# First tiles of the output projection and of the merge computed inside the cores, scores and squares in other gaps, an eviction's place, and norms' halves added on GpSimd

## What is computed

```
hn = rms_norm(h, ln_mix[0]);  h += gdn_mixer(hn)            # gated delta rule, 8 heads
h += swiglu(rms_norm(h));     h += ple gate                 # PLE = p @ w * sigmoid(rms_norm(h) @ w)
k, v = shared_kv(h);          h += sb_mixer(rms_norm(h))    # stick-breaking attention, 8 heads
h += swiglu(rms_norm(h));     h += ple gate
x = h;  x += 0.5 * swiglu(rms_norm(x))
y_hy = hyena_branch(...)      # filters from a small MLP, divided by their norm, DFT as matmuls
y_rw = rwkv7_branch(...)      # token shift, recurrence per head in both directions, group norm, gate
x += (sigmoid(g_hy) * y_hy @ hy_out + sigmoid(g_rw) * y_rw @ rw_out) @ w_out
x += 0.5 * swiglu(rms_norm(x));  out = rms_norm(x)
```

## Time and profile before

| what | value |
|---|---|
| time, median of 3 runs | 3155.7 us (3154.51 to 3155.88) |
| profiled execution, its own time | 3157.63 us |
| its span, first to last instruction | 3155.8 us |
| PE busy | 2996.7 us, 95% of the span |
| DVE, ACT, POOL busy | 48%, 34%, 7% |
| chain that ended last, by engine | PE 81%, DVE 5%, ACT 4%, issue 2% |
| mean granted TensorE clock | 0.98 |

### The profile page before, as it was taken

The page is one execution under the profiler, slowest core; times in us unless marked ns, Lnnn a source line. Parts: engine busy times, 40 slices in busy tenths (PEclk is TensorE's granted clock), DMA queues, the critical chain, the costliest instruction groups (busy, mean ns, idle before and its releaser), DMA issues.

```text
span 3155.8 us, 46998 instructions
## 1 busy us (share of the span) xinstructions
PE 2996.7 (95%) x21374; PEld 2461.1 (78%) x21374; DVE 1502.1 (48%) x1435; ACT 1058.5 (34%) x1115; POOL 215.8 (7%) x125
## 2 busy tenths in 40 slices
PE   8988889999999889999999999989998998999998
PEld 6767768888788778888878888768877887788886
DVE  6654534443354444443354434445567664544432
ACT  4453333222344333222342222432244332232221
POOL 1002100000000000000010000320002211000000
PEclk9999989999999999999999999989999999999999
DMA  3210012223222102222322223312230002122222
GB/s 137 80 57 2 2 54 94 93 94 114 98 92 84 51 15 93 102 99 100 107 88 99 94 95 117 104 44 90 77 126 4 3 5 111 67 94 102 99 94 80
DMA packets 44758, 249.29 MB, mean 79 GB/s; under 512 B 8428, under 2 KB 12268, under 8 KB 16913
## 3 DMA queue, kind: packets, MB, share of 16 engines
q1 hardware_dynamic: 43408, 242.11, 21.8%
q10 hardware_dynamic: 1152, 4.19, 0.3%
HBM read 237.90 MB, written 8.39 MB: 78 GB/s over the span
## 4 chain that ended last, share of the span: by engine, by line
PE 81%; DVE 5%; ACT 4%; issue 2%; POOL 0%; DVEq 0%; ACTq 0%
PE ps L560 65%; PE ps L2613 7%; PE ps L1319 2%; PE ps L1947 1%; PE ps L2223 1%; PE ps L2207 1%; ACT whi L265 1%; DVE wlo L271 1%; DVE gdn_XX L1661 0%; PE ps L3396 0%; PE ps L2799 0%; PE ps L1379 0%; DVE sb_sp L3496 0%; ACT sb_la L3470 0%; PE ps L1470 0%
## 5 line engine op out<-in xcount | busy, mean ns | idle before, releaser
L271 DVE TENSOR_TENSOR wlo<-wraw,whi 128x2048 fp32r<-128x2048 f32 x210 | 487.0, 2320 | 1000.3 <-ACT whi L265 1000.1
L265 ACT ACTIVATE whi<-wraw 128x2048 fp32r<-128x2048 f32 x210 | 402.1, 1915 | 1006.1 <-PE ps L560 1006.1
L560 PE MATMUL ps<-ffn_xh,whi 128*128 128x512 f32 x1408 | 550.4, 391 | 2.2 <-DVE ffn_xl L380 2.1
L560 PE MATMUL ps<-ffn_xh,wlo 128*128 128x512 f32 x1408 | 552.2, 392 | 0.0
L560 PE MATMUL ps<-ffn_xl,whi 128*128 128x512 f32 x1408 | 549.5, 390 | 0.0
L560 PEld LDWEIGHTS ps<-ffn_xh,whi 128*128 128x128 f32 x1408 | 264.4, 188 | 60.3 <-DVE ffn_xl L380 2.5
L560 PEld LDWEIGHTS ps<-ffn_xl,whi 128*128 128x128 f32 x1408 | 264.3, 188 | 60.0 <-issue 0.7
L560 PEld LDWEIGHTS ps<-ffn_xh,wlo 128*128 128x128 f32 x1408 | 264.5, 188 | 55.7
L560 PE MATMUL ps<-ffn_uh,wlo 128*128 128x512 f32 x704 | 275.9, 392 | 0.0
L560 PE MATMUL ps<-ffn_uh,whi 128*128 128x512 f32 x704 | 275.5, 391 | 0.0
L560 PE MATMUL ps<-ffn_ul,whi 128*128 128x512 f32 x704 | 274.2, 389 | 0.0
(11 more groups left out here) (494 smaller groups left out, 4747.9 us busy)
## 6 DMA issues: line engine op xcount, KB each, us to landing
wraw<-in_weights SPq DMA_DIRECT2D x212, 1024.0 KB, 4.8
gates_kept<-gates_tmp ACTq DMA_DIRECT2D x8, 512.0 KB, 4.1
mix_gate<-gates_kept SPq DMA_DIRECT2D x8, 512.0 KB, 11.2
h<-in_x SPq DMA_DIRECT2D x4, 512.0 KB, 7.9
mix_y<-hz_kept SPq DMA_DIRECT2D x2, 1024.0 KB, 5.9
out<-out SPq DMA_DIRECT2D x4, 512.0 KB, 2.7
ple_raw<-in_p SPq DMA_DIRECT2D x4, 256.0 KB, 5.1
hy_decay<-in_hy_decay SPq DMA_DIRECT2D x4, 256.0 KB
```

The source lines that it names most:

```text
L265: c.nc.scalar.activation(c.whi[:, j % 2, :], c.wraw[:, j % 2, :], ACT.Copy).then_inc(c.hi_ready, 1)
L271: c.nc.vector.tensor_tensor(c.wlo[:, j % 2, :], c.wraw[:, j % 2, :], c.whi[:, j % 2, :].bitcast(F32), ALU.subtract).then_inc(c.lo_ready, 1)
L560: last = nc.tensor.matmul(pair[:, m, :], a, b, start=opens and n == 0 and wa + xa == 0, stop=closes and n == len(ks) - 1 and wa == 1)
```

## The change

Seven parts.

1. **Norms.** After the last accumulation POOL adds the two halves of `norm_acc` (a new 128x512 addition, `one`), in all ten norms. `pe_sum` waits for it and multiplies one half instead of two; in `kv_n` four sums per token instead of eight.
2. **Units.** `Dense.tensor` is cut into units (three matmuls of one 128-wide block of one k), which `tensor_ahead` can issue from another part. `skip_group` twice keeps the parity of the PSUM pairs for `gdn_out`.
3. **Gated delta rule.** In stage GP slots 8 to 19 issue one unit each of tile 0 of `gdn_out` (heads 0 to 5), stage GP+1 slots 1 to 4 three units each of tile 1: 24 units. The casts of the two held tiles move from slots 6 and 12 of stage GP to slots 1 and 3.
4. **Hyena filter.** The squares of the second filter on ACT move from after the last tile of `project` to beside tile 4 and early in tile 5; PE sums them after tile 0 of `gates` instead of halfway through it.
5. **Recurrence.** The last slots of DVE's preparation of pair 0 (19 and on) move from tile 6 to tile 7 of `shift`, behind the last eviction.
6. **Merge.** In the last stage of `Recurrence` 14 of the 16 units of the merge's tile 0 are issued, 6 at slot 0, 3 at 17, 3 at 19, 2 at 21.
7. **Attention.** Scores and softplus of heads 0 and 1 stand beside tiles 2 and 3 of `v_part`; the core's loop starts at head 0. `o` and `w` get other places in SBUF.

```diff
+def skip_group(c):
+    c.freed[c.groups] = c.freed[c.groups - 2]
+    c.groups += 1
...
+            if q == (2 if self.direct else 3):
+                pool.wait_ge(*self.Q.at(f"{name}.acc{q}"))
+                nc.gpsimd.tensor_tensor(b.acc[:, 0, :], b.acc[:, 0, :], b.acc[:, 1, :], ALU.add)\
+                    .then_inc(*self.Q.done(f"{name}.one"))
...
-        pe.wait_ge(*self.Q.at(f"{name}.acc{2 if self.direct else 3}"))
+        pe.wait_ge(*self.Q.at(f"{name}.one"))
...
-        for m in range(2):
-            last = nc.tensor.matmul(c.ps[:, 4, :], c.ones[:, :], b.acc[:, m, :], start=m == 0,
-                                    stop=m == 1 and not self.direct)
+        last = nc.tensor.matmul(c.ps[:, 4, :], c.ones[:, :], b.acc[:, 0, :], start=True, stop=not self.direct)
...
+    def tensor_ahead(self, pe, r, end):
+        for unit in self.units(r)[self.begun.get(r, 0):end]:
+            self.pe_unit(pe, r, *unit)
+        self.begun[r] = end
...
# DeltaCore.tensor, .scalar, .vector
+                if stage == GP and 8 <= s < 20:
+                    self.out.tensor_ahead(pe, 0, s - 7)
+                elif stage == GP + 1 and 1 <= s < 5:
+                    self.out.tensor_ahead(pe, 1, (3, 6, 9, 12)[s - 1])
...
-                if stage == GP and s in (6, 12):
-                    ring_lo(c, dve, self.j_held - 2 + s // 12)
+                if stage == GP and s in (1, 3):
+                    ring_lo(c, dve, self.j_held - 2 + s // 3)
...
# HyenaFilters
+            self.act_square(act, 1, 0)
+            self.act_square(act, 1, 1)
         elif r == 5:
-            for q in range(NH):
-                self.act_square(act, 1, q)
+            self.act_square(act, 1, 3)
             self.act_norm(act, 1)
...
     def tensor_halfway(self, pe, r):
-        if r == 0:
-            f.pe_squares(pe, 1)
...
# Recurrence
+                if k == HP + 1 and s in (0, 17, 19, 21):
+                    self.merge.tensor_ahead(pe, 0, {0: 6, 17: 9, 19: 12, 21: 14}[s])
...
-        for s in {3: range(8), 4: range(8, 12), 5: range(12, 17), 6: range(17, SLOTS)}.get(r, ()):
+        for s in {3: range(8), 4: range(8, 12), 5: range(12, 17), 6: range(17, 19), 7: range(19, SLOTS)}.get(r, ()):
...
# StickCore (the same on ACT and DVE)
+    def tensor_beside(self, pe, r):
+        if r >= 2:
+            self.pe_scores(pe, r - 2)
...
-        for i in range(-1, HEADS + 1):
-            if i + 1 < HEADS:
+        for i in range(HEADS + 1):
+            if 2 <= i + 1 < HEADS:
                 self.pe_scores(pe, i + 1)
```

More of the change, by code:

```diff
@@ L352, in __init__ @@
         self.E.plan([f"{name}.sum"] + ([f"{name}.sumT"] if rows else []))
-        self.Q.plan([f"{name}.acc{q}" for q in range(1, 3 if direct else 4)])
+        self.Q.plan([f"{name}.acc{q}" for q in range(1, 3 if direct else 4)] + [f"{name}.one"])
     def act_pair(self, act, q):
@@ L407, in pe_sum @@
             for n in range(T // P):
-                for m in range(2):
-                    last = nc.tensor.matmul(c.ps[:, 5, n:n + 1], b.acc[:, m, n * P:(n + 1) * P], c.ones[:, 0:1],
-                                            start=m == 0, stop=m == 1)
+                last = nc.tensor.matmul(c.ps[:, 5, n:n + 1], b.acc[:, 0, n * P:(n + 1) * P], c.ones[:, 0:1], start=True, stop=True)
             last.then_inc(*self.E.done(f"{name}.sumT"))
@@ L472, in __init__ @@
         c.groups += n
+        self.begun, self.seen = {}, set()
         self.plan()
@@ new lines, in units @@
+    def units(self, r):
+        out = []
+        for q, opens, closes, ks in self.body[r]:
+            if self.tokens_out:
+                order = [(m, n) for m in range(T // P) for n in range(len(ks))]
+            else:
+                order = [(m, n) for n in range(len(ks)) for m in range(WN // P)]
+            out += [(q, opens, closes, ks, m, n, at == 0, at == len(order) - 1) for at, (m, n) in enumerate(order)]
+        return out
+    def tensor_ahead(self, pe, r, end):
+        for unit in self.units(r)[self.begun.get(r, 0):end]:
+            self.pe_unit(pe, r, *unit)
+        self.begun[r] = end
@@ new lines, in pe_unit @@
+    def pe_unit(self, pe, r, q, opens, closes, ks, m, n, first, final):
+        c, nc, j = self.c, self.c.nc, self.j0 + r
+        t, pair, (kw, kx) = j % 2, self.pair(q), ks[n]
+        if first and q == self.body[r][0][0]:
+            pe.wait_ge(c.lo_ready, j + 1)
+        if first and opens and self.g0 + q - 2 in c.freed:
+            pe.wait_ge(*c.freed[self.g0 + q - 2])
+        if self.tokens_out:
+            pair = pair.rearrange("p b (a n) -> p (b a) n", n=WN)
+        x = self.x_of(q, kx)
+        for what in self.x_ready(q, kx) if self.x_ready else []:
+            if what not in self.seen:
+                self.seen.add(what)
+                pe.wait_ge(*what)
+        for wa, xa in ((0, 0), (0, 1), (1, 0)):
+            w = (c.whi, c.wlo)[wa]
+            if self.tokens_out:
+                a, b = x[xa][:, m * P:(m + 1) * P], w[:, t, kw * WN:(kw + 1) * WN]
+            else:
+                a, b = w[:, t, kw * WN + m * P:kw * WN + (m + 1) * P], x[xa]
+            last = nc.tensor.matmul(pair[:, m, :], a, b, start=opens and n == 0 and wa + xa == 0,
+                                    stop=closes and n == len(ks) - 1 and wa == 1)
+        if self.k_freed and r == len(self.body) - 1 and m == WN // P - 1 and n < len(ks) - 1:
+            last.then_inc(*self.E.done(f"{self.name}.k{n}"))
+        if final:
+            if q == self.body[r][-1][0]:
+                last.then_inc(c.tile_done, 1)
+            elif closes:
+                self.pe_closed(last, q)
@@ L567, in tensor @@
+    def tensor(self, pe):
+        for r in range(len(self.body)):
+            units = self.units(r)
+            for at in range(self.begun.get(r, 0), len(units)):
+                if 2 * at == len(units):
+                    for b in self.halfway:
+                        b.tensor_halfway(pe, r)
+                self.pe_unit(pe, r, *units[at])
             if r == 0 and self.norm:
@@ L1968, in scalar_early @@
             self.act_damp(act, 1, 2)
+        elif r == 5:
+            self.act_square(act, 1, 2)
     def scalar_beside(self, act, r):
@@ L3416, with __init__ @@
     OFF = {0: 512, 2: 896, 1: 1024}
-    def __init__(self, c, k, q, v, o, v_part, norms, at, mats_at):
+    def __init__(self, c, k, q, v, o, v_part, norms, at, last_at, mats_at):
         self.c, self.k, self.q, self.v, self.o, self.v_part, self.norms = c, k, q, v, o, v_part, norms
@@ L3425, in __init__ @@
         self.ls = [c.at(f"sb_ls{n}", [P, w], at + (3 + n) * size) for n in range(2)]
-        self.w = [c.at(f"sb_w{n}", [P, w], at + (5 + n) * size) for n in range(2)]
+        self.w = [c.at(f"sb_w{n}", [P, w], place) for n, place in enumerate((at + 5 * size, last_at))]
         self.z = c.ps[:, 4:7, :].rearrange("p b t -> p (b t)")
@@ L3756, in first_half @@
                      beside_pe=(norms[2],))
-    o = two(c, "sb_o", KD, 20544, 73728)
-    core = StickCore(c, k, q, v, o, v_part, norms[2], 36928, 18432)
+    o = two(c, "sb_o", KD, 20544)
+    core = StickCore(c, k, q, v, o, v_part, norms[2], 53312, 102464, 18432)
+    v_part.beside = v_part.beside_pe = (norms[2], core)
     first = [out] + parts + [ple, StickTables(core, k_part.j0), k_part, q_part, v_part, core]
@@ L3797, in second_half @@
                   (c.at("mix_mh", [P, KD, T], 107264, F32R), c.at("mix_ml", [P, KD, T], 32768, F32R)))
+    core.merge = merge
     out = Residual(c, "mix_out", simple(4), merge.m_of, merge.m_ready)
```

68 lines of the change are left out of this document (21 added, 47 removed).

## The result

The changed kernel takes 3133.6 us (median of 4 runs, 3131.2 to 3138.3) beside 3155.8 us before: a ratio of 0.9928, 95% interval 0.9916 to 0.9940. That is 22 us faster where 36.5 were forecast, and outside the range of 3106 to 3131. The profiled execution has its own time of 3138.25 us and a span of 3136.5 us.

What follows compares the result with a forecast made beforehand. PE was taken as the bound, busy in 95% of the span. Gains of 4.5 + 8 + 11.5 + 1 + 9.5 + 2 = 36.5 us from 3157.6 gave 3121.1, so 3119 for the median; range 3106 to 3131.

Steps and rivals of the forecast that it cites:

- Attention, 8 us: Attention core: heads 0 and 1 start beside v_part's tiles, so head 2 comes earlier; gain 8 us (5.5 to 9.5).
- Squares, 11.5 us: Hyena filter and gates: earlier squares shorten PE's 13.6 us wait in gates' tile 0; gain 11.5 us (9.5 to 14.1).
- Merge, 9.5 us: Merge after the recurrence: only two units of tile 0 remain behind the last mix_y; gain 9.5 us (7 to 11).
- Recurrence, 1 us: Recurrence's first matmuls: earlier eviction starts PE sooner, but rw_XT still waits for DVE; gain 1 us (0 to 2.8).
- Norms, 2 us: All ten norms: one fp32 sum saved on PE against POOL's new addition; net gain 2 us (-2 to 8.6).
- the nearest row is a POOL operation of that size at 1.4 us: Norms: basis for pricing POOL's new 128x512 addition, taken from a profiled operation of equal size.
- 0.7 lost: At kv_n: only 1.13 us free, addition late by up to 3, sums halved (-0.9); net loss 0.7 us.
- 2 lost: At ffn2_n: PE already waits, so the addition of 1.3 to 3.4 us stands bare against 0.86 saved; loss 2 us.
- so the addition hides and 6 x 0.86 come in: At six norms the last accumulation ends at least 4.75 us before PE's sum, so 5.2 us are gained.
- Projection, 4.5 us: Output projection behind the delta core: 24 early units use PE's idle time; gain 4.5 us (2 to 7.7).
- I let it come 4.4 us later, at 450: Projection: the last pair's gdn_ol, ready at 445.6 before, was put at 450 (447 to 452) with PE filled.
- the second one: Rival, chance 0.21: early units paid at the lower clock, POOL stands against DVE; 3128 to 3137 us.

Runs made afterwards that it cites:

- e4: Changed kernel with one of tile 1's 12 early gdn_out units between the last pair's two sums of squares, eleven behind the second; 3128.6 us, ratio 0.9902.
- e3: Changed kernel with its delta core part undone: no early gdn_out units, held casts at slots 6 and 12, no skip_group; 3131.8 us, ratio 0.9916.
- e14: The changed kernel again, nothing altered, one more profiled execution; span 3130.9 us.
- e1: Changed kernel without its norms part: pe_sum multiplies both halves again, no POOL addition; 3125.8 us, ratio 0.9895.
- e6: Changed kernel with its second skip_group in front of sb_out instead of behind gdn_out; 3131.0 us, ratio 0.9919.
- e7: The kernel before the change with the norms part alone added; 3161.7 us over 10 runs, ratio 1.0015.
- e8: Changed kernel with the old attention core, scores of head 0 behind the values' last tile; 3141.4 us, ratio 0.9951.
- e5: Changed kernel with the POOL addition in all norms but kv_n, ffn2_n and hy_n; 3122.6 us, ratio 0.9893.

## Why the prediction was wrong, point by point

- **Attention, 8 us:** right. The |z| of head 2 stands at 1075.57 in the changed kernel, which had come 3.06 us late to this part: 8.0 earlier by the same count. Another 2 us came behind that: in the core the granted clock was low for 6.8 us, before for 17.0, and the spacing of three tiles of sb_out gave 0.6. This extra is not a property of the code: over the fourteen profiled executions that have the new core the stretch gained 7.7 (e4) to 11.6 us (e3), the more the shorter the clock was low in it.

```profile
1063.19 1.24 ACT L3502 ACTIVATE sb_la<-ps 128x1280 f32<-128x1280 f32 x1 [0.28 <-PE ps L3579]
...
1075.57 1.22 ACT L3502 ACTIVATE sb_la<-ps 128x1280 f32<-128x1280 f32 x1
...
1066.52 0.76 PE L3595 MATMUL ps<-sb_sp,sb_mats 128*128 128x128 f32 x2 [3.36 <-DVE sb_v L890]
```

- **Squares, 11.5 us:** right; 11.6 up to the second tile of gates, and 1.7 more behind it. The changed kernel came 4.4 us late to this place, so its times are read less 4.4: the last addition on POOL ended at 2109.16 + 2.34 = 2111.5, that is 2107.1, at the far end of 2105 to 2107.4, and tile 0 at 2108.4, that is 2104.0, where 2103.7 was said. The 2.1 us on top of 2105 are one meeting with DVE: the first addition took 4.47 us and not 2.4, behind the cast at 2099.18. (The upper end is mis-added: as far as it can be redone, 2110.9 holds the lower level's 3.6 us for the sums, not the upper's, and 2125.26 - 2110.9 is 14.4.)

```profile
2099.18 2.85 DVE L271 TENSOR_TENSOR wlo<-wraw,whi 128x2048 fp32r<-128x2048 f32 x1 [4.23 <-ACT whi L265]
...
2099.83 4.47 POOL L2134 TENSOR_TENSOR hy_sq<-hy_sq,hy_sq 128x1024 f32<-128x1024 f32 x1
...
2109.16 2.34 POOL L2134 TENSOR_TENSOR hy_sq<-hy_sq,hy_sq 128x1024 f32<-128x1024 f32 x1 [1.23 <-ACT hy_sq L2061]
...
2111.55 3.57 PE L1962 MATMUL ps<-ones,hy_sq 128*128 128x1 f32 x16 [3.17 <-POOL hy_sq L2134]
...
2118.07 0.47 PE L573 MATMUL ps<-hy_xh,whi 128*128 128x512 f32 x1
```

- **Merge, 9.5 us:** right at 9.9. Its first tile ends 1.7 us after the last `mix_y`, with the granted clock at 1.00 from 2660 to 2684. **Recurrence, 1 us:** nearer to nothing, as said.
- **Norms, 2 us:** this term failed; it was -8.3 in e14's stretches, and without the part (e1) the kernel is 7.9 us faster. Three steps of it. First, "the nearest row is a POOL operation of that size at 1.4 us": with a cast on DVE ahead of it the addition took 3.2, at nine norms of ten, so the 3.4 that stood as the far end was the rule, and the sign of being wrong that the prediction named (over 3 us at places with slack) came true, 3.23 at ffn0_n. I had the exclusion of POOL and DVE from the earlier trace rows but put it on DVE's side; here DVE came first, and POOL lost. Second, "0.7 lost" and "2 lost" counted the wait and not the lower clock behind it. At kv_n the loss follows how long the clock was low: 0.5 us in e6, where it stayed up (1.00 from 915 to 930), 2.1 in e3, e4 and e7, where it was low for 3.4 us, 3.7 to 3.9 in the other seven, with 6.8 us. So the wait alone was priced rightly, and the clock had no term. At ffn2_n it was 4.7 to 5.0 with 6.8 us low, 2.0 in e7 and e8 with 3.4. Third, "so the addition hides and 6 x 0.86 come in" took the six places as ends of their own. The six additions did hide and the 5.2 came in, but the 0.86 at hy_n turned the race in the filter: 5.0 lost in e14, 3.3 of it with the race and 1.7 by the lower clock, which stands there without it too (e5).
- **Projection, 4.5 us:** failed, -0.1 measured. Its sum gave 4.9, and three things were missing. "I let it come 4.4 us later, at 450": by the core's own count the last pair's `gdn_ol` came 5.7 later (at 452.3, the changed kernel being 1.0 late there already), because six units stood in front of the second sum, at the lower clock for half of them; the sum had the units' amount but not their order among the core's own steps on PE. That is 1.3. Behind the wait for it PE ran at the lower clock for 3.4 us, which the sum did not have: from `gdn_ol` to tile 3's eviction it took 31.2 us (452.3 to 483.5) and not 29.1, most of these 2.1 by the clock. And `skip_group` was named as keeping the parity and given no price: 1.6. Order alone undoes all three (e4 and e6), and the part is then worth 5.9 us (84.4 against 90.3).
- **The rule of the Trainium skill** (SBUF — State Buffer, section Terms): the trace agrees with it, 3.19 us for an addition that takes 1.29 with nothing beside it. Taken as I read it for the other side (a loss of some 5 for the part on the norms) it was nearer than the sum: e7 is 5 us slower. But the way there was another: that loss was DVE's time behind POOL, the measured one is POOL's behind DVE and the clock. That the loser is blocked, whichever it is, was in the rule, and I asked only who would be held by POOL.
- **The rivals:** what happened is nearest to the second one (0.21), 3128 to 3137, in its half on POOL against DVE. That its number holds is in part luck. Of the four losses it priced (8.5 at the projection, 2 at the squares, 4 at the norms, 2.5 at attention) those at squares and attention did not come, the norms' was over twice as large, and the projection's 4.6 had other causes: its early units ran at the upper clock for most of the way. In 417 to 441 the granted clock is 0.78, where it was 0.51.

```profile
417.00:441.00 24.00, 20.77 (x94) 17.01 (x94) 7.22 (x14) 4.83 (x7) 0.00 (x0) 0.78 0.20 81
```
